# A chain of small elementwise steps placed on GpSimd instead of VectorE, in a two-layer hybrid decoder kernel

## The chip, the cores and the metric

The kernel runs on one core of one Trainium2 chip. The core's engines work side by side and wait for each other by semaphores: TensorE (PE in the profile) multiplies matrices, VectorE (DVE), ScalarE (ACT) and GpSimd (POOL) do elementwise work, SyncE (SP) issues transfers. The metric is the device time of one execution, in microseconds (us).

## The reference

One inference step of two layers, over a prompt of 512 tokens and 8 sequences of 4 new tokens, 1024 wide. In each layer the normalized input is multiplied by `w_in`, the columns of the product go to four mixers (SSD, retention, GLA, RG-LRU), their outputs through `w_out`, and a SwiGLU follows. The change touches how the SSD mixer gets its log decays, and two factors of the RG-LRU:

```python
dt = jax.nn.softplus(dt_raw.astype(jnp.float32) + p['ssd_dt_bias'].astype(jnp.float32))
log_a = -dt * jnp.exp(p['ssd_a_log'].astype(jnp.float32))
...
log_a = -LRU_C * r.astype(jnp.float32) * jax.nn.softplus(-p['lru_lambda'].astype(jnp.float32))
```

The kernel computes softplus(x) as max(x, 0) + log(1 + e), where e = exp(-|x|), and the logarithm as 2z(1 + z²/3 + z⁴/5 + ...) with z = e/(2 + e), up to z¹⁴/15. All of it is on tiles of 128 rows by 19 columns: 16 step sizes of the prompt's four chunks, one of the samples, two of the RG-LRU.

## The kernel before

Tokens lie along the free axis: 512 of the prompt and 32 samples, in two halves of 272. Weights come in units of 1024 x 128 (`NUNIT` = 101 a layer; 25 are `w_in`, `IN_UNITS`). Each unit is multiplied in fp32 precision from rounded parts, three matmuls for each of 8 slices and each half, all on L1238 (`unit_half`), so 24 matmuls make one half of one unit. A half stands in one of three PSUM banks until DVE has emptied it (`dense_free`).

A unit's weights need preparing in a ring of three. SP loads `raw` (L362). ACT rounds it to `wh` (L404). The rest `wl` is made in one of two ways: for units 3 to 24 of each layer (`ON_VECTOR`), ACT writes -wh to `wl` (L406, `negated`) and POOL issues an accumulating transfer of the same weights onto it (L383, `lo_added`). For the others POOL subtracts (L376). POOL walks the units in order and does nothing else.

The 25 units of `w_in` make 50 slots, two a unit (a unit and its half). Each engine goes through the slots in the same order: PE multiplies the half, DVE empties it (`evacuate`; for units 1 to 6 that is `conv`, a causal convolution, L717 to L735), ACT prepares the weights of the unit three ahead (`hi_ahead`). Between them stand the mixers' stages, by a table written out by hand (`SLOTS`). Three matter here:

- `dt` in slot 5. PE turns the step sizes (L1249, L1252), DVE adds the bias (L786 to L789, `sp_in`), ACT makes exp(-|x|) (L448 to L452, `sp_exp`), and DVE does the whole rest, L792 to L820, with a drain after each dependent step, and signals `dt_ready`.
- `gla_cum` in slot 9: DVE's L907 and the scans of L910.
- `ssd_a` of chunk 0 in slot 12: PE waits for `dt_ready` and `conv_silu`, then does L1315 and what follows. ACT's exponentials and DVE's L852 come after PE there.

Slot 6 begins with unit 3's first half. PE's next use of the bank that this half stands in, slot 9, needs DVE's L719 of slot 6, which is behind all of `dt` on DVE.

Of the kernel before, what the change touches and what calls it, by code (L numbers as in the profile page):

```python
# [25 lines left out]
ALU = mybir.AluOpType  # L26
ACT = mybir.ActivationFunctionType
F32 = mybir.dt.float32
F32R = mybir.dt.float32r

P = 128
# [37 lines left out]
NUNIT = REST0 + 2 * REST + KT  # L69
# [10 lines left out]
def splits(n):  # L80

    layer, u = divmod(n, NUNIT)
    vector = layer * len(ON_VECTOR) + min(max(u - 3, 0), len(ON_VECTOR))
    return (u in ON_VECTOR, vector + 1 if u in ON_VECTOR else n - vector)
# [89 lines left out]
def trunk(nc, weights, params, consts, x, s_ssd, s_ret, s_gla, y, o_conv, o_ssd, o_ret, o_gla, o_lru,  # L174
          n_ssd, n_ret, n_gla):
    with ExitStack() as ctx:
        def sb(name, cols, dt=F32, parts=P):
            return ctx.enter_context(nc.sbuf_tensor(name, [parts, *cols], dt))

        def sem(name):  # L180
            return ctx.enter_context(nc.semaphore(name))

        def signal(name, per_layer, start=0):
            return Signal(sem(name), per_layer, start)


        h = sb("h", [KT, TOK])
# [8 lines left out]
        sp_x, sp_a, sp_e, sp_z = (sb(n, [19]) for n in ("sp_x", "sp_a", "sp_e", "sp_z"))  # L196
        sp_2, sp_p, sp_m, sp_y = (sb(n, [19]) for n in ("sp_2", "sp_p", "sp_m", "sp_y"))
        ssd_rate, log_a, st_log_a = sb("ssd_rate", [5]), sb("log_a", [4, 4]), sb("st_log_a", [1])
        log_a_hi, log_a_lo = sb("log_a_hi", [4, 4], F32R), sb("log_a_lo", [4, 4], F32R)
        st_e, st_mask = sb("st_e", [2 * NSEQ + 2]), sb("st_mask", [NSEQ])  # L200
        lru_neg, lru_pos = sb("lru_neg", [2]), sb("lru_pos", [2])
# [58 lines left out]
        def par(name, i=0, n=1):  # L260
            at, _ = PARAM[name]
            return pr[:, at + i:at + i + n]
# [32 lines left out]
        act_lo = signal("act_lo", FT)  # L295

        dt_out, dt_turned, sp_in, sp_exp = (signal(n, 1) for n in ("dt_out", "dt_turned", "sp_in", "sp_exp"))
        dt_ready = signal("dt_ready", 1)
        conv_done = signal("conv_done", 6)
        conv_silu = signal("conv_silu", 4)  # L300
        ssd_a, ssd_e, ssd_dx, ssd_bin, ssd_b, ssd_s = (
# [44 lines left out]
        @block.sync  # L346
        def _(sp):
            sp.dma_start(raw[:, 0, :], weights[0]).then_inc(raw_loaded[0], 16)
            for i in range(KT // 2):
                sp.dma_start(h[:, 2 * i:2 * i + 2, :], x[:, 2 * i:2 * i + 2, :]).then_inc(x_loaded[i], 16)  # L350
            sp.wait_ge(x_loaded[1], 16)
            sp.dma_start(raw[:, 1, :], weights[1]).then_inc(raw_loaded[1], 16)
            sp.wait_ge(x_loaded[KT // 2 - 1], 16)
            sp.dma_start(raw[:, 2, :], weights[2]).then_inc(raw_loaded[2], 16)
            sp.dma_start(S1[:, 0:NEXACT], consts[:, NCONST + KT:NCONST + KT + NEXACT]).then_inc(exact_loaded, 16)
            sp.wait_ge(first_lo, 1)
            sp.dma_start(raw[:, 0, :], weights[3]).then_inc(raw_loaded[0], 16)
            sp.dma_start(cs[:], consts[:, 0:NCONST]).then_inc(consts_loaded, 16)
            for n in range(1, ALL - RING):
                vector, count = splits(n)  # L360
                sp.wait_ge(negated if vector else lo_done, count)
                sp.dma_start(raw[:, n % RING, :], weights[n + RING]).then_inc(raw_loaded[n % RING], 16)  # L362
            for s in range(RING):
                sp.wait_ge(raw_loaded[s], 16 * len(range(s, ALL, RING)))
            for i in range(KT // 2):
                sp.wait_ge(y_final, 2 * i + 2)
                sp.dma_start(y[:, 2 * i:2 * i + 2, :], h[:, 2 * i:2 * i + 2, :]).then_inc(y_stored, 16)
            sp.wait_ge(y_stored, 16 * (KT // 2))
            sp.wait_ge(stored, DEPTH * STORES)


        @block.gpsimd
        def _(pool):
            def split(s, n):
                pool.wait_ge(hi_done, n + 1)
                nc.gpsimd.tensor_tensor(wl[:, s, :], raw[:, s, :], wh[:, s, :].bitcast(F32),  # L376
                                        ALU.subtract).then_inc(lo_done, 1)

            for n in range(1, ALL):
                vector, count = splits(n)  # L380
                if vector:
                    pool.wait_ge(negated, count)
                    nc.gpsimd.dma_start(wl[:, n % RING, :], weights[n], accum_op=ALU.add).then_inc(lo_added[n % RING], 16)  # L383
                else:
                    split(n % RING, n)

# [2 lines left out]
        def _(act):  # L389
# [51 lines left out]
            for layer in range(DEPTH):  # L441
# [82 lines left out]
                def gla_b_(c):  # L524
                    _, off, n = CH[c]
                    act.wait_ge(gla_b.sem, gla_b.at(layer, c + 1))
                    for t in range(2):
                        ins = a(gv[:, t, off:off + n], M[2 - t if c < SAMPLE else 2 + t][:, 0:n], ACT.Copy)
                    ins.then_inc(gla_o.sem, 1)
# [123 lines left out]
        def _(dve):  # L653
            v = nc.vector
            tt, ts, stt, copy = v.tensor_tensor, v.tensor_scalar, v.scalar_tensor_tensor, v.tensor_copy
# [45 lines left out]
            for layer in range(DEPTH):  # L701
# [80 lines left out]
                def dt(_=None):  # L782
                    dve.wait_ge(dt_turned.sem, dt_turned.at(layer, 1))
                    dve.wait_ge(consts_loaded, 16)
                    bias = par("dt_bias", 0, 4)
                    tt(sp_x[:, 0:16].rearrange("p (c h) -> p c h", h=4), M[4][:, 0:16].rearrange("p (c h) -> p c h", h=4),  # L786
                       bias.unsqueeze(1).to_broadcast([P, 4, 4]), ALU.add)
                    tt(sp_x[:, 16:17], M[4][:, 16:17], par("dt_bias", 4), ALU.add)
                    ts(sp_x[:, 17:19], par("lru_lambda", 0, 2), -1.0, None, ALU.mult)  # L789
                    dve.drain().then_inc(sp_in.sem, 1)  # L790

                    ts(sp_m[:], sp_x[:], 0.0, None, ALU.max)  # L792
                    dve.wait_ge(sp_exp.sem, sp_exp.at(layer, 1))
                    ts(sp_z[:], sp_e[:], 2.0, None, ALU.add)
                    dve.drain()
                    v.reciprocal(sp_z[:], sp_z[:])
                    dve.drain()
                    tt(sp_z[:], sp_z[:], sp_e[:], ALU.mult)
                    dve.drain()
                    tt(sp_2[:], sp_z[:], sp_z[:], ALU.mult)  # L800
                    dve.drain()
                    ts(sp_p[:], sp_2[:], 1.0 / 15.0, None, ALU.mult)
                    for k in (13, 11, 9, 7, 5, 3):
                        dve.drain()
                        stt(sp_p[:], sp_p[:], 1.0 / k, sp_2[:], ALU.add, ALU.mult)
                    dve.drain()
                    stt(sp_p[:], sp_p[:], 1.0, sp_z[:], ALU.add, ALU.mult)
                    dve.drain()
                    stt(sp_y[:], sp_p[:], 2.0, sp_m[:], ALU.mult, ALU.add)
                    dve.drain()  # L810
                    stt(log_a[:], sp_y[:, 0:16].rearrange("p (c h) -> p c h", h=4), -1.0,
                        ssd_rate[:, 0:4].unsqueeze(1).to_broadcast([P, 4, 4]), ALU.mult, ALU.mult)
                    stt(st_log_a[:], sp_y[:, 16:17], -1.0, ssd_rate[:, 4:5], ALU.mult, ALU.mult)
                    dve.drain()
                    copy(log_a_hi[:], log_a[:])
                    dve.drain()
                    tt(log_a_lo[:], log_a[:], log_a_hi[:].bitcast(F32), ALU.subtract)
                    ts(lru_neg[:], sp_y[:, 17:19], -8.0, None, ALU.mult)
                    ts(lru_pos[:], sp_y[:, 17:19], 8.0, None, ALU.mult)
                    dve.drain().then_inc(dt_ready.sem, 1)  # L820

                def ssd_sample_stacks():
                    group = cst("pair").unsqueeze(1).unsqueeze(3).to_broadcast([P, 2, 2, NS])
# [291 lines left out]
                def ret_out(t):  # L1115
# [3 lines left out]

                stages = {  # L1120
                    "dt": dt, "ssd_a": ssd_a_, "ssd_b": ssd_b_, "lru_scan": lru_scan, "gla_cum": gla_cum,
                    "gla_pre": gla_pre_, "gla_a": gla_a_, "gla_b": gla_b_, "rotate": rotate, "ret_a": ret_a_,
                    "ret_b": ret_b_, "ret_out": ret_out, "z_gate": z_gate, "gla_stat": lambda: norm_rstd(0, 4, 64), "gla_norm": gla_norm_,
# [657 lines left out]
```

## Time and profile before

| | |
|---|---|
| median of 3 runs | 1423.91 us (1422.46 to 1425.79) |
| the profiled execution | 1419.99 us |
| its span, first to last instruction | 1418.2 us |
| PE busy (matmuls) | 1377.8 us, 97% |
| DVE busy | 640.0 us, 45% |
| ACT busy | 496.8 us, 35% |
| POOL busy | 415.5 us, 29% |
| mean granted clock of PE | 0.988 |

Matmuls are pipelined, so a busy PE isn't PE at its peak: the start-to-start distance of its rows says more. Busy shares are means over all stages; what a stage waits for is read in its own stretch of the timeline. Lines are those of the kernel before.

### The profile page before, as it was taken

To read this page: it belongs to the slowest core of one execution; us is meant where nothing else is said; L and a number is where in the kernel's file an instruction comes from. 1 tells how busy PE (TensorE), PEld (TensorE's weight loads), DVE (VectorE), ACT (ScalarE), POOL (GpSimd) and SP (SyncE) were. 2 spreads that over 40 slices of the span, in tenths; PEclk is the share of its full clock that TensorE was granted. 3 is DMA by queue.
4 is the path that set the end of the run, shared out by engine and by line. 5 is a ranking of instruction groups with operands and counts; after the bars stand their busy time and mean duration, and the time that the engine had idled before them with its cause. 6 is when DMAs were issued, how large, how long until landed. Compare 5 with 4: busy or idle time off the path is not lost.

```text
span 1418.2 us, 25863 instructions
## 1 busy us (share of the span) xinstructions
PE 1377.8 (97%) x11237; PEld 1331.4 (94%) x11237; DVE 640.0 (45%) x1230; ACT 496.8 (35%) x685; POOL 415.5 (29%) x205
## 2 busy tenths in 40 slices
PE   6998999999999999999999989999999999999996
PEld 6987888999999999999989878889999999999996
DVE  5744766464331333133756446755433223322334
ACT  5625354433221222122454264543322122212231
POOL 1100001343334444333511000024334444333441
PEclk9999999999999999999999999999999999999998
DMA  7644654222222222232355466423232222332221
GB/s 267 138 98 116 156 118 110 75 75 90 90 90 88 83 86 87 90 90 90 106 146 121 107 145 160 91 79 94 85 90 85 81 89 90 90 90 90 89 91 64
DMA packets 41347, 146.09 MB, mean 103 GB/s; under 512 B 5136, under 2 KB 6160, under 8 KB 41104
## 3 DMA queue, kind: packets, MB, share of 16 engines
q1 hardware_dynamic: 30528, 112.01, 26.2%
q0 software_dynamic: 6336, 23.07, 9.0%
q10 hardware_dynamic: 4368, 9.34, 2.1%
q8 instruction: 89, 1.46, 0.4%
q14 instruction: 26, 0.21, 0.0%
HBM read 136.35 MB, written 5.82 MB: 100 GB/s over the span
## 4 chain that ended last, share of the span: by engine, by line
PE 86%; DVE 5%; ACT 4%; DVEq 1%; DMA 1%; issue 1%; ACTq 1%; POOL 0%; SPq 0%
PE bank L1238 78%; PE bank L1188 1%; DMA wl<-weights 1%; PE bank L1478 1%; ACT wh L404 1%; PE bank L1329 0%; ACT wl L406 0%; PE bank L1204 0%; PE bank L1389 0%; ACT xh L429 0%; PE bank L1484 0%; ACT L487 0%; PE bank L1414 0%; DVE h L1179 0%; PE bank L1199 0%
## 5 line engine op out<-in xcount | busy, mean ns | idle before, releaser
L1238 PE MATMUL bank<-xh,wh 128*128 128x272 f32 x2208 | 651.3, 295 | 13.7 <-DVE xl L692 7.7
L1238 PE MATMUL bank<-xh,wl 128*128 128x272 f32 x2208 | 643.5, 291 | 0.0
L1238 PE MATMUL bank<-xl,wh 128*128 128x272 f32 x2208 | 639.7, 290 | 0.0
L376 POOL TENSOR_TENSOR wl<-raw,wh 128x1024 fp32r<-128x1024 f32 x157 | 377.0, 2402 | 590.7 <-ACT wh L404 574.8
L404 ACT ACTIVATE wh<-raw 128x1024 fp32r<-128x1024 f32 x199 | 210.8, 1059 | 693.1 <-PE bank L1238 672.2
L1238 PEld LDWEIGHTS bank<-xh,wh 128*128 128x128 f32 x2208 | 420.3, 190 | 20.9 <-issue 15.9
L1238 PEld LDWEIGHTS bank<-xl,wh 128*128 128x128 f32 x2208 | 421.1, 191 | 1.1 <-issue 0.5
L1238 PEld LDWEIGHTS bank<-xh,wl 128*128 128x128 f32 x2208 | 419.8, 190 | 0.0
L1157 DVE TENSOR_TENSOR tz<-bank,rs_bcast 128x272 f32<-128x272 f32 x176 | 77.5, 441 | 293.3 <-PE bank L1238 289.2
L1137 DVE TENSOR_TENSOR h<-h,bank 128x272 f32<-128x272 f32 x128 | 55.3, 436 | 215.8 <-PE bank L1238 215.8
L383 POOL DMA_DIRECT2D wl<-weights x44 | 38.3, 870 | 385.5 <-ACT wl L406 385.5
L1238 PE MATMUL bank<-gh_gla,wh 128*128 128x272 f32 x256 | 73.9, 289 | 1.0 <-DVE gl_gla L1165 1.0
L1238 PE MATMUL bank<-gh_ret,wl 128*128 128x272 f32 x256 | 74.4, 290 | 0.0
L1238 PE MATMUL bank<-gl_gla,wh 128*128 128x272 f32 x256 | 73.9, 289 | 0.0
L1238 PE MATMUL bank<-gh_ssd,wl 128*128 128x272 f32 x256 | 73.9, 289 | 0.0
L1238 PE MATMUL bank<-gl_ssd,wh 128*128 128x272 f32 x256 | 73.9, 289 | 0.0
L1238 PE MATMUL bank<-gh_ssd,wh 128*128 128x272 f32 x256 | 73.9, 289 | 0.0
L1238 PE MATMUL bank<-gh_gla,wl 128*128 128x272 f32 x256 | 73.8, 288 | 0.0
L1238 PE MATMUL bank<-gh_ret,wh 128*128 128x272 f32 x256 | 73.5, 287 | 0.0
L1238 PE MATMUL bank<-gl_ret,wh 128*128 128x272 f32 x256 | 73.4, 287 | 0.0
L672 DVE TENSOR_TENSOR sq_sum<-sq_sum,Vx 128x544 f32<-128x544 f32 x30 | 61.4, 2048 | 4.6 <-issue 1.3
L1238 PE MATMUL bank<-gh_lru,wl 128*128 128x272 f32 x192 | 55.9, 291 | 0.0
(360 smaller groups left out, 1763.2 us busy)
## 6 DMA issues: line engine op xcount, KB each, us to landing
raw<-weights SPq DMA_DIRECT2D x202, 512.0 KB, 3.6
wl<-weights POOLq DMA_DIRECT2D x44, 512.0 KB, 7.6
h<-x SPq DMA_DIRECT2D x4, 544.0 KB, 6.0
y<-h SPq DMA_DIRECT2D x4, 544.0 KB, 2.7
cs<-consts SPq DMA_DIRECT2D x1, 1336.5 KB, 8.2
rv<-rk ACTq DMA_DIRECT2D x8, 136.0 KB, 5.8
tz<-rq ACTq DMA_DIRECT2D x8, 136.0 KB, 4.7
S<-s_ssd ACTq DMA_DIRECT2D x2, 512.0 KB, 4.3
```

The lines of the kernel that those rows point to most:

```text
L376: nc.gpsimd.tensor_tensor(wl[:, s, :], raw[:, s, :], wh[:, s, :].bitcast(F32), ALU.subtract).then_inc(lo_done, 1)
L383: nc.gpsimd.dma_start(wl[:, n % RING, :], weights[n], accum_op=ALU.add).then_inc(lo_added[n % RING], 16)
L404: a(wh[:, s, :], raw[:, s, :], ACT.Copy).then_inc(hi_done, 1)
L672: tt(sq_sum[:], sq_sum[:], sq[:, m % 2, :], ALU.add).then_inc(sq_added.sem, 1)
L1137: ins = tt(h[:, m, cols], h[:, m, cols], acc, ALU.add)
L1157: tt(tz[:, i // 2, cols], acc, rs_bcast[:, cols], ALU.mult).then_inc(dense_free.sem, 1)
L1188: return nc.tensor.transpose(out, src, exact("ident", n_in, 0, n_in).bitcast(F32))
L1238: ins = mm(bank_, wt[:, n % RING, w], xx[:, cols], start=(i == 0 and j == 0), stop=(i == len(ks) - 1 and j == 2))
L1478: ins = mm(M[4][0:n, at:at + 2], sq[:, t, off:off + n], cst("pair"), start=True, stop=True)
```

## The change

ScalarE's part of `dt` stays. VectorE keeps the bias, 2 + e, and the reciprocal, and signals `sp_recip`. Everything behind that, and max(x, 0), is done by GpSimd in a new function `step_sizes`, called once a layer: right behind the transfer issue of unit 6, so ahead of the wait and issue for unit 7. The fused steps of VectorE (`scalar_tensor_tensor`, one instruction) are two instructions on GpSimd, an add or a multiply by a constant and one of two tensors. Its last drain signals `dt_ready`.

```diff
--- before.py
+++ after.py
@@ -295,7 +295,7 @@
         act_lo = signal("act_lo", FT)
 
         dt_out, dt_turned, sp_in, sp_exp = (signal(n, 1) for n in ("dt_out", "dt_turned", "sp_in", "sp_exp"))
-        dt_ready = signal("dt_ready", 1)
+        dt_ready, sp_recip = signal("dt_ready", 1), signal("sp_recip", 1)
         conv_done = signal("conv_done", 6)
         conv_silu = signal("conv_silu", 4)
         ssd_a, ssd_e, ssd_dx, ssd_bin, ssd_b, ssd_s = (
@@ -376,11 +376,47 @@
                 nc.gpsimd.tensor_tensor(wl[:, s, :], raw[:, s, :], wh[:, s, :].bitcast(F32),
                                         ALU.subtract).then_inc(lo_done, 1)
 
+            def step_sizes(layer):
+                pool.wait_ge(sp_in.sem, sp_in.at(layer, 1))
+                nc.gpsimd.tensor_scalar(sp_m[:], sp_x[:], 0.0, None, ALU.max)
+                pool.wait_ge(sp_recip.sem, sp_recip.at(layer, 1))
+                nc.gpsimd.tensor_tensor(sp_z[:], sp_z[:], sp_e[:], ALU.mult)
+                pool.drain()
+                nc.gpsimd.tensor_tensor(sp_2[:], sp_z[:], sp_z[:], ALU.mult)
+                pool.drain()
+                nc.gpsimd.tensor_scalar(sp_p[:], sp_2[:], 1.0 / 15.0, None, ALU.mult)
+                for k in (13, 11, 9, 7, 5, 3):
+                    pool.drain()
+                    nc.gpsimd.tensor_scalar(sp_p[:], sp_p[:], 1.0 / k, None, ALU.add)
+                    pool.drain()
+                    nc.gpsimd.tensor_tensor(sp_p[:], sp_p[:], sp_2[:], ALU.mult)
+                pool.drain()
+                nc.gpsimd.tensor_scalar(sp_p[:], sp_p[:], 2.0, 2.0, ALU.mult, ALU.add)
+                pool.drain()
+                nc.gpsimd.tensor_tensor(sp_p[:], sp_p[:], sp_z[:], ALU.mult)
+                pool.drain()
+                nc.gpsimd.tensor_tensor(sp_y[:], sp_p[:], sp_m[:], ALU.add)
+                pool.drain()
+                nc.gpsimd.tensor_scalar(sp_m[:], sp_y[:], -1.0, None, ALU.mult)
+                pool.drain()
+                nc.gpsimd.tensor_tensor(log_a[:], sp_m[:, 0:16].rearrange("p (c h) -> p c h", h=4),
+                                        ssd_rate[:, 0:4].unsqueeze(1).to_broadcast([P, 4, 4]), ALU.mult)
+                nc.gpsimd.tensor_tensor(st_log_a[:], sp_m[:, 16:17], ssd_rate[:, 4:5], ALU.mult)
+                pool.drain()
+                nc.gpsimd.tensor_copy(log_a_hi[:], log_a[:])
+                pool.drain()
+                nc.gpsimd.tensor_tensor(log_a_lo[:], log_a[:], log_a_hi[:].bitcast(F32), ALU.subtract)
+                nc.gpsimd.tensor_scalar(lru_neg[:], sp_y[:, 17:19], -8.0, None, ALU.mult)
+                nc.gpsimd.tensor_scalar(lru_pos[:], sp_y[:, 17:19], 8.0, None, ALU.mult)
+                pool.drain().then_inc(dt_ready.sem, 1)
+
             for n in range(1, ALL):
                 vector, count = splits(n)
                 if vector:
                     pool.wait_ge(negated, count)
                     nc.gpsimd.dma_start(wl[:, n % RING, :], weights[n], accum_op=ALU.add).then_inc(lo_added[n % RING], 16)
+                    if n % NUNIT == 6:
+                        step_sizes(n // NUNIT)
                 else:
                     split(n % RING, n)
 
@@ -788,36 +824,11 @@
                     tt(sp_x[:, 16:17], M[4][:, 16:17], par("dt_bias", 4), ALU.add)
                     ts(sp_x[:, 17:19], par("lru_lambda", 0, 2), -1.0, None, ALU.mult)
                     dve.drain().then_inc(sp_in.sem, 1)
-
-                    ts(sp_m[:], sp_x[:], 0.0, None, ALU.max)
                     dve.wait_ge(sp_exp.sem, sp_exp.at(layer, 1))
                     ts(sp_z[:], sp_e[:], 2.0, None, ALU.add)
                     dve.drain()
-                    v.reciprocal(sp_z[:], sp_z[:])
-                    dve.drain()
-                    tt(sp_z[:], sp_z[:], sp_e[:], ALU.mult)
-                    dve.drain()
-                    tt(sp_2[:], sp_z[:], sp_z[:], ALU.mult)
-                    dve.drain()
-                    ts(sp_p[:], sp_2[:], 1.0 / 15.0, None, ALU.mult)
-                    for k in (13, 11, 9, 7, 5, 3):
-                        dve.drain()
-                        stt(sp_p[:], sp_p[:], 1.0 / k, sp_2[:], ALU.add, ALU.mult)
-                    dve.drain()
-                    stt(sp_p[:], sp_p[:], 1.0, sp_z[:], ALU.add, ALU.mult)
-                    dve.drain()
-                    stt(sp_y[:], sp_p[:], 2.0, sp_m[:], ALU.mult, ALU.add)
-                    dve.drain()
-                    stt(log_a[:], sp_y[:, 0:16].rearrange("p (c h) -> p c h", h=4), -1.0,
-                        ssd_rate[:, 0:4].unsqueeze(1).to_broadcast([P, 4, 4]), ALU.mult, ALU.mult)
-                    stt(st_log_a[:], sp_y[:, 16:17], -1.0, ssd_rate[:, 4:5], ALU.mult, ALU.mult)
-                    dve.drain()
-                    copy(log_a_hi[:], log_a[:])
-                    dve.drain()
-                    tt(log_a_lo[:], log_a[:], log_a_hi[:].bitcast(F32), ALU.subtract)
-                    ts(lru_neg[:], sp_y[:, 17:19], -8.0, None, ALU.mult)
-                    ts(lru_pos[:], sp_y[:, 17:19], 8.0, None, ALU.mult)
-                    dve.drain().then_inc(dt_ready.sem, 1)
+                    v.reciprocal(sp_z[:], sp_z[:]).then_inc(sp_recip.sem, 1)
+
 
                 def ssd_sample_stacks():
                     group = cst("pair").unsqueeze(1).unsqueeze(3).to_broadcast([P, 2, 2, NS])
```

POOL's order in the build, after the change, layer 0, with the semaphores that it waits for (`sp_2` is printed as `sp`):

```order
L376 TENSOR_TENSOR wl<-raw,wh 128x1024 [waits hi_done] x2
L417 DMA wl<-weights 128x1024 [waits negated] x4
L381 TENSOR_SCALAR sp_m<-sp_x 128x19 [waits sp_in]
L383 TENSOR_TENSOR sp_z<-sp_z,sp_e 128x19 [waits sp_recip]
L385 TENSOR_TENSOR sp<-sp_z 128x19
L387 TENSOR_SCALAR sp_p<-sp 128x19
L390 TENSOR_SCALAR sp_p<-sp_p 128x19
L392 TENSOR_TENSOR sp_p<-sp_p,sp 128x19
...
L408 TENSOR_TENSOR log_a_lo<-log_a,log_a_hi 128x16
L409 TENSOR_SCALAR lru_neg<-sp_y 128x2
L410 TENSOR_SCALAR lru_pos<-sp_y 128x2
L417 DMA wl<-weights 128x1024 [waits negated] x18
```

Before, the issues of all 22 units followed each other (`L383 DMA ... x22`); now 26 instructions stand behind the fourth.

DVE's order before, from the bias in slot 5 to the evacuation in slot 6:

```order
L789 TENSOR_SCALAR sp_x<-pr 128x2
L792 TENSOR_SCALAR sp_m<-sp_x 128x19
L794 TENSOR_SCALAR sp_z<-sp_e 128x19 [waits sp_exp]
L796 RECIPROCAL sp_z<-sp_z 128x19
L798 TENSOR_TENSOR sp_z<-sp_z,sp_e 128x19
...
L819 TENSOR_SCALAR lru_pos<-sp_y 128x2
L717 MEMSET cbuf 128x3 [waits dense_done]
L718 COPY cbuf<-pr 128x8x3
L719 TENSOR_TENSOR cbuf<-bank,rs_bcast 128x272
```

and after:

```order
L825 TENSOR_SCALAR sp_x<-pr 128x2
L828 TENSOR_SCALAR sp_z<-sp_e 128x19 [waits sp_exp]
L830 RECIPROCAL sp_z<-sp_z 128x19
L753 MEMSET cbuf 128x3 [waits dense_done]
L754 COPY cbuf<-pr 128x8x3
L755 TENSOR_TENSOR cbuf<-bank,rs_bcast 128x272
```

Eighteen instructions have left DVE between the reciprocal's neighbourhood and the evacuation, which now follows the reciprocal at once.

## Rows read from the trace of the kernel before

**Rows 1.** Page, the chain that ended last: share of the span by engine
```profile
PE 86%; DVE 5%; ACT 4%; DVEq 1%; DMA 1%; issue 1%; ACTq 1%; POOL 0%; SPq 0%
```

**Rows 2.** Timeline of DVE, layer 0: start us, duration us, instruction, [idle before <- releaser]
```profile
44.61 0.17 DVE L794 TENSOR_SCALAR sp_z<-sp_e 128x19 f32<-128x19 f32 x1 [2.21 <-ACT sp_e L452]
...
44.86 0.28 DVE L796 RECIPROCAL sp_z<-sp_z 128x19 f32<-128x19 f32 x1
...
45.21 0.18 DVE L798 TENSOR_TENSOR sp_z<-sp_z,sp_e 128x19 f32<-128x19 f32 x1
...
49.05 0.18 DVE L718 COPY cbuf<-pr 128x24 f32<-128x24 f32 x1
```

**Rows 3.** Timeline of PE, layer 0, around unit 4's second half and at chunk 1
```profile
48.85 0.28 PE L1238 MATMUL bank<-xh,wl 128*128 128x272 f32 x1
...
49.62 0.39 PE L1238 MATMUL bank<-xh,wh 128*128 128x272 f32 x1 [0.49 <-DVE cbuf L719]
...
73.33 0.66 PE L1315 MATMUL bank<-cx,log_a 128*64 128x128 f32 x8 [0.71 <-DVEq L883]
```

**Rows 4.** Chain of waits in layer 1: start us, length us, what
```profile
724.89 8.49 DMA wl<-weights
...
740.41 18.30 PE bank L1238 x144
```

**Rows 5.** Timeline of DVE, layer 1: its waits for PE
```profile
743.65 0.41 DVE L722 TENSOR_TENSOR cbuf<-bank,rs_bcast 128x240 f32<-128x240 f32 x1 [2.00 <-PE bank L1238]
...
762.16 0.42 DVE L852 TENSOR_TENSOR V<-bank,sp_y 128x256 f32<-128x256 f32 x1 [1.34 <-PE bank L1188]
```

**Rows 6.** Timeline of POOL: the transfer issues of unit 6, layers 0 and 1
```profile
50.98 0.86 POOL L383 DMA_DIRECT2D wl<-weights  x1 [10.26 <-ACT wl L406]
...
746.96 0.88 POOL L383 DMA_DIRECT2D wl<-weights  x1 [13.51 <-ACT wl L406]
```

**Rows 7.** L383, transfers issued at 56.46, then at 752.04 (unit 7)
```profile
DMA to landing us min/median/max: 8.1/8.1/8.1
...
DMA to landing us min/median/max: 7.5/7.5/7.5
```

**Rows 8.** Timeline of PE: start of ssd_a(0) and of unit 7
```profile
61.89 0.44 PE L1315 MATMUL bank<-cx,log_a 128*64 128x128 f32 x4
...
69.25 0.47 PE L1238 MATMUL bank<-xh,wh 128*128 128x272 f32 x1
...
758.64 0.66 PE L1315 MATMUL bank<-cx,log_a 128*64 128x128 f32 x8
...
765.99 0.47 PE L1238 MATMUL bank<-xh,wh 128*128 128x272 f32 x1
```

**Rows 9.** One line each: instruction xcount: duration ns min/median/max, first and last start
```profile
L376 POOL TENSOR_TENSOR wl<-raw,wh x157: 2372/2398/2671, 14.0 to 1389.5; 128x1024 fp32r<-128x1024 f32 x157
...
L842 DVE TENSOR_TENSOR Vx<-S,st_e x2: 1224/1224/1225, 112.9 to 809.6; 128x1024 f32<-128x1024 f32 x2
...
L1757 POOL MEMSET const-float32-0.0<- x1: 98/98/98, 0.2 to 0.2; 128x1 f32 x1
...
L684 DVE MEMSET sp_x<- x1: 74/74/74, 0.8 to 0.8; 128x19 f32 x1
```

**Rows 10.** Timelines of DVE, then POOL, where two-input work meets L376
```profile
479.46 0.72 DVE L1162 TENSOR_TENSOR tz<-tz 128x544 f32<-128x544 f32 x1 [0.44 <-issue]
...
480.91 2.12 DVE L1165 TENSOR_TENSOR gl_ssd<-tz,gh_ssd 128x544 fp32r<-128x544 f32 x1 [0.73 <-ACT gh_ssd L635]
...
479.77 2.67 POOL L376 TENSOR_TENSOR wl<-raw,wh 128x1024 fp32r<-128x1024 f32 x1 [3.64 <-ACT wh L404]
```

**Rows 11.** Timeline of DVE, layer 0: the fourth convolution's passes
```profile
55.23 2.58 DVE L735 SCALAR_TENSOR_TENSOR ct<-cbuf,pr,ct 128x568 f32<-128x568 f32 x3
```

**Rows 12.** Timeline of PE; then a stretch: us, busy by engine, PEclk, DMA share, GB/s
```profile
32.70 0.59 PE L1238 MATMUL bank<-xh,wh 128*128 128x272 f32 x1 [2.50 <-DVE cbuf L719]
...
32.70:36.00 3.30, 3.30 (x14) 3.30 (x15) 2.99 (x8) 0.00 (x0) 0.00 (x0) 0.50 1.01 243
```

## The prediction

> **What bounds the kernel now.** I read the page first: the chain that ended last is TensorE (PE) for 86% of the span, almost all of it on the matmuls of L1238, with VectorE (DVE) on 5% [rows 1]. So an edit on DVE or GpSimd (POOL) moves the time only where PE waits, and I looked for those places around the `dt` stage of each layer, in the list of waits, then in the timelines of PE, DVE and POOL, then in the chain of waits. The median of the runs is 1423.91 us; the profiled execution took 1419.99 us (span 1418.2), 3.9 below it. The sum is made against that execution, and 3.9 is added for the median. A change of under 0.2% (2.85 us) can't be told from none here.
>
> In layer 0, DVE does the chain from L798 to L819 between 45.21 and 49.05 us, and only then empties the bank that PE needs [rows 2]. PE issues a matmul every 0.125 us; here it goes from 48.85 to 49.62, so it loses 0.77 - 0.12 = 0.65 us [rows 3]. In layer 1 it loses nothing: it waits for a transfer until 733.38 and from 740.41 computes 144 matmuls without a break, up to `ssd_a` [rows 4], and DVE, through with the chain, waits 2.00 us for PE at L722 [rows 5].
>
> **What the change removes.** 18 DVE instructions a layer, 3.84 us of the timeline in layer 0. In layer 0 PE then waits for nothing at that bank: **-0.65 us**. Beyond that DVE is early for nothing: it waits for PE again soon. In layer 1: **0**. The reciprocal and the wait for ScalarE's exponential (2.21 us, [rows 2]) stay on DVE, ahead of the bank.
>
> **What it adds: a chain on POOL.** It stands behind the transfer issue of unit 6 and ahead of that of unit 7. It has two kinds of wait, for `sp_in` and `sp_recip`; both are met some 6 us before POOL gets there (DVE's reciprocal ends at 45.14; the issue of unit 6 starts at 50.98, held by ScalarE [rows 2, 6]). So the chain starts at 50.98 + 0.86 = 51.84, and in layer 1 at 746.96 + 0.88 = 747.84. ScalarE's work before it doesn't come from DVE's chain, so I leave these as they are.
>
> Two things wait for its end. PE's `ssd_a(0)` waits for `dt_ready`: PE is there at 61.89, or 61.24 with the 0.65 gained, and in layer 1 at 758.64 [rows 8]. That leaves **9.4 and 10.8 us**. The transfer of unit 7, queued behind on POOL, takes 8.1 us from issue to landing in layer 0 and 7.5 in layer 1 [rows 7], and PE starts that unit at 69.25 - 0.65 = 68.60 and at 765.99 [rows 8]. It must be issued by 60.5 and 758.5, so the chain may take **8.7 and 10.65 us**. The unit after is needed a whole unit of PE later and has the room. SP's queue waits on ScalarE's `negated`, not on POOL, so the raw loads don't move.
>
> How long is the chain? 26 instructions a layer, of which 22 follow each other with a drain between and 4 don't. The trace has no small two-sided instruction on POOL. Bounds for one drained step: from below, a POOL MEMSET of 0.10 us plus the 0.08 that DVE leaves between drained instructions (44.61 + 0.17 to 44.86), 0.18. From above, POOL takes 2.40 us for 1024 elements; if it ran at DVE's pace (1.22 - 0.18 us for 1005 more elements, 1.04 ns each), 1.33 us of that would be fixed, so about 1.4 [rows 2, 9]. That end is not likely: the whole ratio of POOL to DVE at 1024 elements is 2.40/1.22 = 1.96, which makes of DVE's 0.18 us some 0.35, and 0.43 with the gap; the MEMSETs (98 against 74 ns) have a ratio of 1.3, which makes 0.31. I take 0.36, between but nearer to the small forms, as these are small. With a MEMSET's 0.1 for each of the other four, 22 x 0.36 + 4 x 0.1 = **8.3 us** with nothing in the way.
>
> Something is in the way. At 479.77 the POOL instruction of L376 took 2.67 us instead of 2.40, when DVE had begun one with two SBUF inputs 0.31 us before; and the next of DVE's, L1165, took 2.12 us beside it, where the same shape at L1162 took 0.72 [rows 9, 10]. Whoever comes second waits for the first to end. In the chain's window DVE has such work: three passes of L735 for 2.58 us [rows 11], L907 and the scans of L910, and L732 before them; in layer 0 they now follow PE's unit 4 closely and so come a little earlier than in these rows, but still in the window. During L735's passes (one each 0.86 us) POOL gets about one step in each, and loses 3 x (0.86 - 0.36) = 1.5 us; I give L732, L907 and the five scans 0.7 together. Bounds: 0, and the 1.5 twice (the next convolution follows) with 0.2 for each of those seven, about 4.4. I take 2.2, and the chain lasts **10.5 us**.
>
> The Trainium skill says the same of this place (SBUF — State Buffer, "SBUF: two separate sides"): the pair of ports that VectorE and GpSimd share is locked for a whole instruction, and the other blocks. It speaks against the move; the trace agrees, with the 2.67 against 2.40 us. Without the rule the chain would be the 8.3 us above and the sum -0.65.
>
> **The sum.** Layer 0: the chain ends at 51.84 + 10.5 = 62.34, 1.10 after PE wants it. Unit 7's transfer is issued then and lands at 70.45; PE, late by 1.10, comes at 69.70 and waits 0.75. -0.65 + 1.10 + 0.75 = +1.2. Layer 1: the chain ends at 758.34, before 758.64; the transfer lands at 765.85, before 765.99: 0. DVE itself may lose up to 0.3 us for each instruction that meets a POOL step; it has the 3.84 us in layer 0, and in layer 1 it still waits 1.34 us for PE at L852 [rows 5], so 0. Total **+1.2 us**: 1421.2 for an execution like the profiled one, a median of **1425.1**.
>
> **The rivals.**
> *The chain is hidden whole.* If it takes under 8.7 us, all that is left is -0.65: 1423.3. For it: 0.31 a step and 1.0 for DVE's work give 8.2. Against: the 2.67 and 2.12 us [rows 10]. Chance 0.15.
> *The chain is the new bound (slower).* Place: PE at `ssd_a(0)` in both layers. From 11.4 us on (a step of 0.40 with the 2.2 for DVE) it costs over 2.85 us. At a step of 0.47 the chain is 13 us: layer 0 pays 64.84 - 61.24 = 3.6, 0.75 and -0.65; layer 1 pays 2.2 and 0.15 for the transfer. That is 6.1, and after the PE wait of 2.50 us before 32.70 the granted clock was 0.50, the lower level, for 3.3 us, with 14 matmuls, which take 1.75 us at 0.125 each [rows 12], so about 1.6 more in layer 0: +7.7, 1431.6. For it: the ratio 1.96 gives 0.43 already. Chance 0.27.
> *A cost at the first use.* POOL has run no TENSOR_SCALAR nor CAST before layer 0's chain. A one-off start, if there is one, adds to layer 0 alone, a microsecond of PE for each. Nothing in the rows prices it; as long as POOL's longest instruction, 2.67 us [rows 9], it makes +3.9, 1427.8. Against: the first TENSOR_TENSOR on POOL, at 14.0, is within the 2.37 to 2.67 us of all 157 [rows 9]. Chance 0.06. The Trainium skill (GPSIMD Engine Reference, "Instruction dispatch") puts the first call of a freshly loaded kernel at about 6 us with no row of its own; by that figure the sum would be some +7, an estimate near 1431. No run here shows it.
> *DVE's freed time is worth more.* DVE is also waited for at the next chunk (PE's 0.7 us at L1315 on DVE's L883, [rows 3]). If an early DVE removes that in both layers too, -0.65 - 2 x 0.7 = -2.05: 1421.9. Against: DVE waits for PE at L722 just before, so it isn't late with old work. Chance 0.04.
> The forecast itself, a chain of 8.7 to 11.4 us, has 0.45; 0.03 is for what I don't see.
>
> **How the numbers follow.** The forecast's band runs from -0.65 to +2.85, 1423.3 to 1426.8. The range takes in the hidden case with the spread of the three runs below it, and the slow chain at 13 us: 1422.0 to 1432.0. Slower by over 0.2%: the 0.27, most of the first-use case (0.04) and the top of the forecast's band with measurement (0.04), 0.35. Faster: 0.05. Same: 0.60.
>
> **What would show it.** On POOL: the distance from sp_m's first to lru_pos' last row (10.5 us), the step between two sp_p rows (0.36 where DVE is idle, about 0.85 beside L735's passes). On DVE: the bank of the third convolution emptied before PE asks, no PE wait near 49. On PE: a wait of 1.1 us at L1315 in layer 0 and none in layer 1, and 0.7 at the start of unit 7. I'm wrong if the step on POOL is 0.2 or over 0.45, if the chain doesn't start right behind the issue, or if PE waits at 49 as before.

## The result, and the profile after

| | before | changed |
|---|---|---|
| median | 1423.18 us (1421.59 to 1425.79, 4 runs) | 1446.67 us (1444.58 to 1449.56, 4 runs) |
| profiled execution | 1419.99 us | 1449.56 us |
| its span | 1418.2 us | 1447.7 us |
| mean granted clock of PE | 0.988 | 0.975 |

The changed kernel takes 1.0167 of the time before (95% interval 1.0142 to 1.0192): **23.5 us slower**. The prediction said 1425.1, with 1422.0 to 1432.0 as its range. The profiled execution of the change is the slowest of its four runs, that of before lies 3.2 us below its median, so the two traces differ by 29.6; which part of that is the change is worked out below.

The list of what PE waited for over the whole of the changed kernel has one new name on top:

```profile
PE bank L1326 <- POOLq L411: 15.8, 2, 8.4
...
PE bank L1249 <- DMA wl<-weights: 3.2, 2, 1.6
...
PE bank L1249 <- DVE cbuf L755: 2.5, 1, 2.5
```

(line, what for: us in total, times, longest.) L1326 is `ssd_a(0)`, L1315 before; L411 is the last drain of `step_sizes`. So PE waits twice, once a layer, for the end of the chain, some 8 us each where 1.1 and 0 were predicted. The wait of 0.49 us for VectorE near 49 us [rows 3] is gone: the two waits for `cbuf` (3.0 us before) are one of 2.5, and one of 0.4 us for another part of `cbuf` (L759) has come up, at 37.6 us. The wait of 1.6 us in layer 0 for `wl` is for unit 6's transfer, at 58.79 us; the kernel before had no wait there.

Why the chain ends late is on POOL's timeline in layer 0 (start us, us, instruction, [idle before <- releaser]):

```profile
50.48 0.86 POOL L417 DMA_DIRECT2D wl<-weights  x1 [10.00 <-ACT wl L442]
51.05 0.62 POOL L381 TENSOR_SCALAR sp_m<-sp_x 128x19 f32<-128x19 f32 x1
51.29 0.57 POOL L383 TENSOR_TENSOR sp_z<-sp_z,sp_e 128x19 f32<-128x19 f32 x1
58.96 0.38 POOL L385 TENSOR_TENSOR sp<-sp_z 128x19 f32<-128x19 f32 x1 [7.11 <-issue]
59.50 0.81 POOL L387 TENSOR_SCALAR sp_p<-sp 128x19 f32<-128x19 f32 x1 [0.16 <-issue]
...
62.18 0.27 POOL L390 TENSOR_SCALAR sp_p<-sp_p 128x19 f32<-128x19 f32 x1 [0.16 <-issue]
62.60 0.23 POOL L392 TENSOR_TENSOR sp_p<-sp_p,sp 128x19 f32<-128x19 f32 x1
62.98 0.27 POOL L390 TENSOR_SCALAR sp_p<-sp_p 128x19 f32<-128x19 f32 x1 [0.16 <-issue]
...
69.19 0.22 POOL L410 TENSOR_SCALAR lru_pos<-sp_y 128x2 f32<-128x2 f32 x1
69.99 1.84 POOL L417 DMA_DIRECT2D wl<-weights  x2 [0.58 <-issue]
```

The chain does start right behind unit 6's issue, with the two operations that have no drain ahead of them, L381 and L383. Then comes the first drain of the chain (L384), and the square z^2 behind it starts **7.11 us** after L383's end. The later drains leave 0.14 to 0.16 us (one in layer 1 leaves 0.46). Layer 1 has the same hold at the same place:

```profile
762.19 0.57 POOL L383 TENSOR_TENSOR sp_z<-sp_z,sp_e 128x19 f32<-128x19 f32 x1
770.45 0.22 POOL L385 TENSOR_TENSOR sp<-sp_z 128x19 f32<-128x19 f32 x1 [7.69 <-issue]
...
781.21 0.22 POOL L410 TENSOR_SCALAR lru_pos<-sp_y 128x2 f32<-128x2 f32 x1
```

"issue" says that the engine waited for nothing that this view shows; drains have no row in it. In the record of single instructions the drain at L384 lasts 8.32 us in layer 0. What ends near it is unit 6's transfer. Its issue at 50.48 answers with:

```profile
DMA to landing us min/median/max: 8.2/8.2/8.2
```

which is 58.7, and z^2 starts at 58.96. That made the first theory.

PE after the stall, in stretches (us, busy by engine, granted clock, DMA share, GB/s):

```profile
66.00:72.00 6.00, 2.49 (x12) 1.98 (x13) 0.00 (x0) 0.00 (x0) 4.08 (x13) 0.50 0.09 7
72.00:78.00 6.00, 6.00 (x28) 5.56 (x27) 1.94 (x5) 1.11 (x4) 0.00 (x0) 0.50 0.88 168
78.00:84.00 6.00, 6.00 (x44) 5.62 (x43) 3.04 (x8) 2.01 (x2) 0.87 (x1) 0.86 0.13 12
```

The granted clock is at its lower level, 1.2 GHz, until about 80 us. The same work, from the start of `ssd_a(0)` to that of unit 7, took 7.36 us before and takes 11.96 here.

**Where the 23.5 us are.** PE's start of `ssd_a(0)` and of unit 7, which before are at 61.89, 69.25 and at 758.64, 765.99 [rows 8], are now

```profile
69.51 1.12 PE L1326 MATMUL bank<-cx,log_a 128*64 128x128 f32 x8 [7.45 <-POOLq L411]
...
81.47 0.48 PE L1249 MATMUL bank<-xh,wh 128*128 128x272 f32 x1
...
781.53 0.69 PE L1326 MATMUL bank<-cx,log_a 128*64 128x128 f32 x4 [8.38 <-POOLq L411]
...
792.57 0.47 PE L1249 MATMUL bank<-xh,wh 128*128 128x272 f32 x1
```

Layer 0: 7.6 us late at `ssd_a(0)`, 12.2 at unit 7; the 4.6 between are the lower clock. PE came to `ssd_a(0)` at 62.06 and not at 61.24; it had waited 1.56 us for unit 6's transfer. Layer 1: by its wait of 8.38 us PE got to `ssd_a(0)` at 773.15, so 14.5 us late, began it 22.9 late and was 26.6 late at unit 7: 12.1 more, 3.7 of them the lower clock. Together the two stages cost **24.3 us**. The other 5 of the 29.6 were not followed row by row. The changed kernel has stretches at the lower clock elsewhere that the profiled execution of before has not, or has shorter (at 141, 199, 909 and 933 us of its own timeline). The version without the chain, which measures as before, has such stretches at the same places of the program, so they aren't charged to the change.

### The profile page after: what moved, and what is told of

Its sections match the earlier page's. It is cut to its first block, busy times and chain, and to the rows that moved or that the text cites. A ratio compares the mean times of both kernels' runs of the same rounds, so it can differ in the third digit from the quotient of the medians.

```text
span 1447.7 us, 25893 instructions
## 1 busy us (share of the span) xinstructions
PE 1390.5 (96%) x11237; PEld 1342.2 (93%) x11237; DVE 634.9 (44%) x1194; ACT 496.9 (34%) x685; POOL 431.3 (30%) x257
## 4 chain that ended last, share of the span: by engine, by line
PE 84%; DVE 5%; ACT 4%; issue 2%; DVEq 1%; POOLq 1%; ACTq 1%; DMA 1%; POOL 0%; SPq 0%
PE bank L1249 74%; PE bank L1199 1%; PE bank L1489 1%; PE bank L1340 1%; ACT wh L440 1%; DMA wl<-weights 1%; ACT wl L442 1%; PE bank L1400 0%; PE bank L1215 0%; PE bank L1326 0%; PE bank L1495 0%; ACT xh L465 0%; POOLq L391 0%; POOLq L389 0%; DVE h L1190 0%
## 5 line engine op out<-in xcount | busy, mean ns | idle before, releaser
L1249 PE MATMUL bank<-xh,wh 128*128 128x272 f32 x2208 | 654.1, 296 | 14.7 <-DVE xl L728 7.7
L376 POOL TENSOR_TENSOR wl<-raw,wh 128x1024 fp32r<-128x1024 f32 x157 | 376.7, 2400 | 591.1 <-ACT wh L440 575.1
```

Source lines behind the costliest of these rows:

```text
L1249: ins = mm(bank_, wt[:, n % RING, w], xx[:, cols], start=(i == 0 and j == 0), stop=(i == len(ks) - 1 and j == 2))
```

## The experiments

The theories they were set against:

- **A**: a drain on GpSimd ends only when the transfer issued ahead of it on GpSimd has landed.
- **B**: code of GpSimd is loaded at its first use; in its second form, **B'**, the first drain behind an issue costs a fixed 7 us.
- **C**: GpSimd is busy with the transfer's descriptors for some us behind the issue.
- **D**: the chain is simply too long, with its 22 steps and the port that it shares with VectorE.

### A drain behind every transfer issue of the kernel before

Behind each of the 44 issues GpSimd drains and writes one column of a tile of its own, so that the drain's end has a row.

```diff
                     nc.gpsimd.dma_start(wl[:, n % RING, :], weights[n], accum_op=ALU.add).then_inc(lo_added[n % RING], 16)
+                    pool.drain()
+                    nc.gpsimd.memset(mark[:], 0.0)
```

> The kernel before, with a drain and a one-column MEMSET on GpSimd behind each of the 44 accumulating transfer issues; VectorE keeps its chain. The MEMSET's row marks when the drain lets go. If a drain on GpSimd waits until the transfer issued ahead of it has landed (theory A), the MEMSETs come 7 to 9 us after each issue, with the 6.2 to 9.8 us that the landings scatter over, in both layers and also in stages where VectorE is idle. If the 7 us of the changed kernel were code fetched at the first use of a new kind of instruction (B), the MEMSETs come within 1.5 us everywhere. If GpSimd is busy writing descriptors (C), they come at 7 us here and in the next kernel too. The time: unit 7's issue in layer 0 moves from 56.5 to about 59 us and is in time, so within 4 us of before; a few of the closer pairs of issues (units 3 and 4) are pushed apart, up to 10 us more by A.

POOL's timeline in layer 0:

```profile
28.38 1.01 POOL L384 DMA_DIRECT2D wl<-weights  x1 [7.33 <-ACT wl L409]
37.68 0.09 POOL L386 MEMSET mark<- 128x1 f32 x1 [8.28 <-issue]
38.12 0.86 POOL L384 DMA_DIRECT2D wl<-weights  x1 [0.35 <-ACT wl L409]
45.64 0.10 POOL L386 MEMSET mark<- 128x1 f32 x1 [6.65 <-issue]
46.08 0.86 POOL L384 DMA_DIRECT2D wl<-weights  x1 [0.35 <-issue]
51.96 0.10 POOL L386 MEMSET mark<- 128x1 f32 x1 [5.01 <-issue]
```

and the landing of the issues at 28.38 and 38.12:

```profile
DMA to landing us min/median/max: 9.1/9.1/9.1
```

```profile
DMA to landing us min/median/max: 7.4/7.4/7.4
```

28.38 + 9.1 = 37.5, 38.12 + 7.4 = 45.5: the MEMSETs stand at 37.68 and 45.64. In the records of single instructions the last landing of each of the 44 issues comes 5.5 to 9.1 us behind the issue, and in all 44 the drain ends 0.07 to 0.08 us after it. A fixed cost couldn't follow the landings over 3.6 us. The drain doesn't wait for SyncE's transfers: one of `raw`, issued at 49.82, took 3.5 us to land, and the drain behind the issue at 46.08 had let go by 51.96. **A holds, D alone falls, and so does B**: there is no chain and no new kind of operation here, and the hold is there each time.

The same MEMSETs without the drain weren't measured, so that C is left to the next version. The time was 1417.37 us in its one run, against 1423.1 (1417.44 to 1427.19, 13 runs) for before: one run shows no cost of 44 such holds, where nothing behind the drain is wanted soon. The issues of units 4 to 8 come late here, and PE waits for none of their transfers.

### The chain without drains

Each drain of the chain is replaced by a semaphore that the operation raises and the next one waits for; the operations and their place stay. The last three raise `dt_ready` themselves, without a drain behind them.

```diff
+            def after_step(ins):
+                stepped[0] += 1
+                ins.then_inc(sp_step, 1)
+                pool.wait_ge(sp_step, stepped[0])
...
-                nc.gpsimd.tensor_tensor(sp_z[:], sp_z[:], sp_e[:], ALU.mult)
-                pool.drain()
-                nc.gpsimd.tensor_tensor(sp_2[:], sp_z[:], sp_z[:], ALU.mult)
-                pool.drain()
+                after_step(nc.gpsimd.tensor_tensor(sp_z[:], sp_z[:], sp_e[:], ALU.mult))
+                after_step(nc.gpsimd.tensor_tensor(sp_2[:], sp_z[:], sp_z[:], ALU.mult))
```

> The changed kernel, with each drain in the chain replaced by a wait on a semaphore that the step before increments; same instructions, same place. A: no hold of 7 us behind the first product, a step of 0.35 to 0.45 us, the chain ends some 9 to 11 us after the issue of unit 6, and PE waits 0 to 2 us at ssd_a(0) in each layer: the time is within 3 us of before. B or C: the hold of 7 us stays and the time stays near 1446. If the chain's length and the shared port are what costs (D), the time stays over 1435.

1431.11 us (1425.55 to 1435.14, 10 runs), 1.005 of before (1.0029 to 1.007): two thirds of the loss are gone, and 8.0 us are left, where A alone had allowed 3. POOL in layer 0:

```profile
51.07 0.86 POOL L415 DMA_DIRECT2D wl<-weights  x1 [10.28 <-ACT wl L440]
...
51.87 0.57 POOL L391 TENSOR_TENSOR sp_z<-sp_z,sp_e 128x19 f32<-128x19 f32 x1
52.52 0.22 POOL L392 TENSOR_TENSOR sp<-sp_z 128x19 f32<-128x19 f32 x1
...
54.67 0.84 POOL L395 TENSOR_SCALAR sp_p<-sp_p 128x19 f32<-128x19 f32 x1
55.59 0.76 POOL L396 TENSOR_TENSOR sp_p<-sp_p,sp 128x19 f32<-128x19 f32 x1
...
58.21 0.27 POOL L395 TENSOR_SCALAR sp_p<-sp_p 128x19 f32<-128x19 f32 x1
58.56 0.23 POOL L396 TENSOR_TENSOR sp_p<-sp_p,sp 128x19 f32<-128x19 f32 x1
58.88 0.27 POOL L395 TENSOR_SCALAR sp_p<-sp_p 128x19 f32<-128x19 f32 x1
...
63.81 0.22 POOL L409 TENSOR_SCALAR lru_pos<-sp_y 128x2 f32<-128x2 f32 x1
```

z^2 follows 0.08 us behind z*e while unit 6's transfer is under way. So GpSimd isn't busy with the transfer: **C falls**, and it is the drain that waits, not the engine. What is left is D: the chain, 51.63 to 64.03, takes **12.4 us**, in layer 1 (748.56 to 761.54) **13.0**, against the 9.4 and 10.8 of room. A step without VectorE is 0.335 us (two from 58.21 to 58.88); ten of the rows in layer 0 take 0.3 to 0.86 us instead of 0.2 to 0.3, together 4.0 us too much, in layer 1 4.5. They stand where VectorE makes its passes of two inputs, so these are the port's. Without them the chain would be 8.4 and 8.5 us long, an estimate from these rows, and would fit both rooms. PE waits for it less than for the drain, but it waits, in layer 0, then in layer 1:

```profile
64.08 0.66 PE L1324 MATMUL bank<-cx,log_a 128*64 128x128 f32 x8 [1.40 <-POOL lru_pos L409]
...
761.59 0.66 PE L1324 MATMUL bank<-cx,log_a 128*64 128x128 f32 x8 [1.86 <-POOL lru_pos L409]
```

Unit 7's transfer, issued at 761.60 and so 3.1 us after the latest time of the prediction, costs nothing: it lands 5.5 us later, before PE comes to that unit at 772.0. The rest is the clock. In layer 1 it is at its lower level for 6.8 us from 763.5 us on, and from `ssd_a(0)` to unit 7 PE takes 10.4 us, 3.1 more than before:

```profile
765.00:778.00 13.00, 11.94 (x78) 10.87 (x77) 6.89 (x17) 3.12 (x6) 0.86 (x1) 0.80 0.62 130
```

### The chain ahead of unit 6's issue

```diff
             for n in range(1, ALL):
                 vector, count = splits(n)
                 if vector:
+                    if n % NUNIT == 6:
+                        step_sizes(n // NUNIT)
                     pool.wait_ge(negated, count)
                     nc.gpsimd.dma_start(wl[:, n % RING, :], weights[n], accum_op=ALU.add).then_inc(lo_added[n % RING], 16)
-                    if n % NUNIT == 6:
-                        step_sizes(n // NUNIT)
```

> The changed kernel with its drains, the chain called ahead of the wait and issue for unit 6 in place of behind it. The transfer in flight is then unit 5's, landed about 3 us after the chain's start in each layer. A: a hold of 3 us, then 8 to 9 us of steps; the chain ends at about 56 us in layer 0 and 749 in layer 1, dt_ready is in time, but unit 6's transfer is issued 5 us late in layer 0 and lands at 63 or 64 where PE wants it at 58: PE waits 4 to 6 us there, 0 to 2 in layer 1: 1428 to 1433 us. B: a hold of 7 us here as well, 1440 or more. C: as A. D: over 1435.

1441.44 us (1437.97 to 1445.7, 4 runs), 1.0142 of before (1.0097 to 1.0186); I had this version too fast. POOL and PE in layer 0:

```profile
43.03 0.23 POOL L383 TENSOR_TENSOR sp_z<-sp_z,sp_e 128x19 f32<-128x19 f32 x1 [2.73 <-DVE sp_z L830]
46.18 0.22 POOL L385 TENSOR_TENSOR sp<-sp_z 128x19 f32<-128x19 f32 x1 [2.92 <-issue]
...
58.37 0.24 POOL L410 TENSOR_SCALAR lru_pos<-sp_y 128x2 f32<-128x2 f32 x1
59.20 2.73 POOL L419 DMA_DIRECT2D wl<-weights  x3 [0.58 <-issue]
```

```profile
64.70 0.57 PE L1249 MATMUL bank<-xh,wh 128*128 128x272 f32 x1 [6.22 <-DMA wl<-weights]
```

The drain holds here too, but for 2.92 us (3.45 in layer 1), since unit 5's transfer is 5.3 us old when z*e ends: A once more, with another unit. The chain then blocks the queue: unit 6 is issued at 59.20, 8.2 us after its time [rows 6], and PE waits 6.22 us for it. `ssd_a(0)` doesn't wait for the chain, and the loss is 18 us against the changed kernel's 23.5. In layer 1 the wait for unit 6's transfer is 4.25 us, where 0 to 2 had been expected: the chain there, begun at 745.59, ends only at 762.05.

### The chain later behind the same issue

The call stands behind the wait for unit 7's `negated`, ahead of its issue.

```diff
                     pool.wait_ge(negated, count)
+                    if n % NUNIT == 7:
+                        step_sizes(n // NUNIT)
                     nc.gpsimd.dma_start(wl[:, n % RING, :], weights[n], accum_op=ALU.add).then_inc(lo_added[n % RING], 16)
-                    if n % NUNIT == 6:
-                        step_sizes(n // NUNIT)
```

> The changed kernel with the chain called behind the wait for unit 7's negation and ahead of unit 7's issue, so that it starts some 4 us later behind unit 6's issue. Theory A (a drain on GpSimd ends when the transfer issued ahead of it has landed): the hold between z*e and z^2 is shorter by as much as the chain starts later, and z^2 begins at the same 59 us in layer 0 and 770.5 us in layer 1 as in the changed kernel; time as the changed kernel, 1441 to 1450 us. Theory B' (a fixed cost of about 7 us of the first drain behind an issue, whatever the age of the transfer): z^2 begins some 4 us later than in the changed kernel, at about 63 us, and the time is 6 to 10 us above the changed kernel. Theory D (the length of the chain alone): no hold at all; excluded if either is seen.

```profile
50.85 0.86 POOL L419 DMA_DIRECT2D wl<-weights  x1 [10.28 <-ACT wl L442]
54.61 0.66 POOL L381 TENSOR_SCALAR sp_m<-sp_x 128x19 f32<-128x19 f32 x1 [2.90 <-ACT wl L442]
55.25 0.22 POOL L383 TENSOR_TENSOR sp_z<-sp_z,sp_e 128x19 f32<-128x19 f32 x1
59.24 0.22 POOL L385 TENSOR_TENSOR sp<-sp_z 128x19 f32<-128x19 f32 x1 [3.77 <-issue]
```

Begun 3.6 us later, the chain is let go at the same time, 59.24 (predicted 59; 58.96 in the changed kernel). The hold is 3.77 us, not 7: **B' falls**. In layer 1 it is 3.17, 9.06 us behind the issue as in the changed kernel (770.45 - 761.38 = 9.07); z^2 stands there at 763.96 and not at the 770.5 expected, as unit 6's issue itself comes 6.5 us earlier (754.90). Time: 1443.13 us in its one run, between the bounds of A.

### What the move could be worth at most

The chain's arithmetic is left out: GpSimd writes constants into its seven results.

```diff
             def step_sizes(layer):
-                pool.wait_ge(sp_in.sem, sp_in.at(layer, 1))
-                nc.gpsimd.tensor_scalar(sp_m[:], sp_x[:], 0.0, None, ALU.max)
                 pool.wait_ge(sp_recip.sem, sp_recip.at(layer, 1))
...
+                for out, value in ((sp_y, 0.01), (log_a, -2.0 ** -7), (st_log_a, -2.0 ** -7), (log_a_hi, -2.0 ** -7), (log_a_lo, 0.0),
+                                   (lru_neg, -0.01), (lru_pos, 0.01)):
+                    nc.gpsimd.memset(out[:].bitcast(F32), value).then_inc(dt_ready.sem, 1)
```

> The changed kernel without the chain's arithmetic: behind unit 6's issue GpSimd writes constants into the seven tiles that the chain made, with one signal each; the computation from step sizes to log decays is left out, so that this is the most that taking the chain from VectorE can be worth. My price of the freed VectorE time is 0.65 us (the bank freed earlier near 49 us in layer 0), so 1422.5 us against 1423.2, within 0.2%. If GpSimd's chain were harmless and the loss came from elsewhere in the change (sp_z and sp_recip handed over, other order), it would be as slow as the changed kernel, 1440 and above. A gain of over 3 us would say that VectorE's chain cost more than the trace showed.

1423.76 us (1420.36 to 1430.85, 12 runs) against 1422.77 (1416.15 to 1429.03, 29 runs), a ratio of 1.0005 (0.9988 to 1.0023). All of the loss is in the chain on GpSimd: the handing over and the new order cost nothing that shows. A chain that cost nothing would bring nothing that can be measured. The chain of waits of its profiled execution (start us, length us, what) has the half microsecond at the bank gone:

```profile
43.43 18.30 PE bank L1221 x144
```

144 matmuls without a break, through the place where PE lost 0.65 us before. So the wait at the bank is gone, as the prediction had it, and what that is worth is too small for twelve runs.

### The same gain without GpSimd

The kernel before, with the chain left on VectorE but put behind the evacuation at slot 6.

```diff
 at_slot(5, "dt")
+at_slot(6, "dt_rest")
...
                     dve.drain().then_inc(sp_in.sem, 1)
 
+                def dt_rest(_=None):
                     ts(sp_m[:], sp_x[:], 0.0, None, ALU.max)
```

> The kernel before, with the chain left on VectorE but moved from slot 5 behind the two operations at slot 6, so that the bank is freed ahead of it. Expected by the trace of before: the 0.49 us wait of PE near 49 us goes, nothing else moves, log decays are ready by about 52 us, 9 us before PE wants them: 1422.5 us, within 0.2% of before. Rival: the later end of the scans behind it costs PE something (the two evacuations at slots 7 and 8 come 3 to 4 us later at most), 1424 to 1426 us.

1423.2 us (1419.63 to 1426.72, 12 runs), 0.9999 of before (0.9985 to 1.0014): no change. The wait near 49 is gone as expected. But the chain of waits has a piece that before didn't have:

```profile
50.49 0.28 issue
50.78 8.01 DMA wl<-weights
58.78 0.14 issue
58.92 1.12 PE bank L1240 x7
```

PE, earlier at unit 6, waits 0.96 us for its transfer. That is issued at 50.78, when ScalarE is through, whatever VectorE does, and took 8.0 us to land; in the changed kernel it took 8.2, and PE lost 1.56 us there, in the version with semaphores 8.2 and 1.14 us. The trace of before had 6.2, the version without the chain 6.4, and neither waited at this unit. Why it takes 6.2 in one execution and 8.2 in another isn't settled by these runs. The median shows no gain, nor the 1 to 3 us of the rival.

### The chain without drains, in two parts around unit 6's issue

From the version with semaphores. Ahead of unit 6's wait and issue stand `sp_m` and the next 13 operations in layer 0, `sp_m` and the next 3 in layer 1; the others stay behind the issue.

```diff
                 if vector:
+                    if n % NUNIT == 6:
+                        first_steps(n // NUNIT)
+                        terms((13, 11, 9, 7, 5) if n < NUNIT else ())
                     pool.wait_ge(negated, count)
                     nc.gpsimd.dma_start(wl[:, n % RING, :], weights[n], accum_op=ALU.add).then_inc(lo_added[n % RING], 16)
                     if n % NUNIT == 6:
-                        step_sizes(n // NUNIT)
+                        terms((3,) if n < NUNIT else (13, 11, 9, 7, 5, 3))
+                        last_steps(n // NUNIT)
```

> The kernel with semaphores in place of drains, and the chain in two parts around unit 6's issue: in layer 0 the first 13 operations ahead of it (GpSimd waits there for 7 us anyway), in layer 1 the first 3 ones. Theory A with the length of the chain as second term (12.4 us in layer 0 and 13.2 us in layer 1 from its first operation to its last, in the run with semaphores, against a room of 9.4 and 10.8 us): layer 0 now fits (8 us left behind the issue) and its PE wait on the chain goes; layer 1 keeps 11.6 us behind the issue and loses about 1 to 2 us; 1423 to 1427 us against 1431.1 with the chain in one piece. If the loss of the version with semaphores were not the chain's length but the issue queue or VectorE's shared port, the split changes nothing: 1429 to 1433 us.

1424.67 us (1418.19 to 1428.07, 10 runs), 1.0012 of before (0.9991 to 1.0032), against 1431.11 in one piece. PE waits for the chain in neither layer: in layer 1, where 1 to 2 us had been expected, what was left ran behind the issue in 9.4 us (747.97 to 757.33), since only about six of its operations met VectorE's passes. That the chain's length against the room was the second term is shown: with the waits for it, 6.4 us of the time went. How much of the length is the steps and how much the port, the split doesn't tell, as both got shorter. That this version is any better or worse than before isn't shown.

## Why the prediction was wrong

It forecast no change that could be told and had 0.35 on slower; the time was 21.6 us above the forecast and 14.7 above the range. Step by step:

- **"So the chain starts at 51.84 ... 8.3 us with nothing in the way" failed.** This step took the drain behind z*e, with the transfer just issued, to cost what DVE's drains cost, 0.08 us. The first of them held for the landing of unit 6's transfer, which moved the rest of the chain to 58.96 and 770.45, 7.1 and 7.7 us late. The landing time was in the prediction, 8.1 us [rows 7], but only as unit 7's price. The kernel before has no drain right behind an issue on GpSimd, so no row could show it; the bounds for one drained step should have had the landing as the upper bound of that first drain, being the one thing pending on the engine. Made so, with the prediction's own 10.5 less its first two operations (0.1 and 0.36), the sum is 50.98 + 8.1 + 10.0 = 69.1 for the chain's end in layer 0 (69.41 measured) and a PE wait of 7.8 (69.1 - 61.24; 7.45 measured). The 4.6 us of lower clock behind it would still be missing.
- **The step of 0.36 us** was 0.40 (62.18 to 62.98 is two): right within what it was given, over 22 steps 0.9 us. The ratio of POOL to DVE (0.43) was the better guide than the MEMSETs (0.31). A drain on GpSimd leaves 0.15 us with nothing in flight, where DVE's 0.08 had been taken.
- **2.2 us for the shared port** was 4.0 and 4.5 in the version where the chain meets the same passes as foreseen. The mechanism is as described: the operations beside L771's passes took 0.68 to 0.81 us. Not three but up to ten operations met them, as the next convolution's passes follow; that was the 4.4 of the upper bound. In the changed kernel itself the port costs less, some 1.6 and 1.8 us, since its PE, and so its VectorE, stands still for most of the chain.
- **The rival "new bound, 13 us, 1431.6"** names what happens without the drains: a chain of 12.4 and 13.0 us that PE waits for in both layers, and a lower clock behind it. That the time, 1431.11, agrees to half a microsecond is luck. The rival's 13 us were steps of 0.47 and 2.2 for the port, measured were 0.335 and 4.0 to 4.5; it had PE waiting 3.6 and 2.2 us for the chain (1.40 and 1.86 measured), 0.9 for unit 7's transfer (none) and 1.6 of lower clock in layer 0 (none there, 3.1 in layer 1), and no wait of 1.14 for unit 6. The kernel that was predicted, with its drains, lies 15.1 us above that rival (1446.67 - 1431.6): the hold and the clock behind it aren't in it.
- **0.75 us for unit 7's transfer** came in no version. Issued late, it landed in 5.4 us (changed kernel) and 5.8 us (semaphores) in layer 0 and not in 8.1, before PE came to the unit.
- **-0.65 us for the bank** was seen at the bank and lost again at unit 6's transfer. The prediction asked only DVE what is late next, and not the transfer behind ScalarE. The two versions made for it measured 1.0 and 0.4 us above before, both within the uncertainty.
- **Layer 1 at 0** failed as layer 0 did, by the same drain: 8.38 us. It would have failed without the drain too, by 1.86 us.
- **1.6 us of half clock** in the rival was 4.6 in layer 0 and 3.7 in layer 1, since PE stood 7 to 8 us and not 2.5. No such term was in the forecast.
- **A first-use cost** wasn't there: the instructions right behind the issue run at once, the version with semaphores runs the same kinds without a hold, and layer 1 has the hold as well. The figure of the Trainium skill (GPSIMD Engine Reference, "Instruction dispatch"), about 6 us for the first call of a freshly loaded kernel, is near the 7.1, and nearness is all that spoke for it.

## What to carry to other kernels

A drain on GpSimd, where that engine also issues transfers, isn't a flush of 0.1 us: it costs what is left of the transfer, up to the 5.5 to 9.1 us here when it stands right behind the issue, and 2.9 to 3.8 when the operation ahead of it ends 4.6 to 5.9 us behind the issue. On GpSimd, order dependent small operations by semaphores (0.335 us a step instead of 0.40, and no hold), or put the drains where nothing is in flight; and when work goes onto an engine that issues transfers, ask which of its instructions wait for everything pending. Before work is moved off an engine for a wait of half a microsecond, look at what PE meets next: leaving the chain out whole brought nothing.

## What was not expected

- The hold itself: 44 of 44 drains ended 0.07 to 0.08 us after the last landing of a transfer of 512 KB, 5.5 to 9.1 us behind its issue. That held with the issue directly ahead. In the three versions with drains inside the chain z^2 starts 0.26 to 0.3 us after the landing in layer 0, and in all three 1.03 us after it in layer 1. Where that last 0.75 us comes from wasn't tried. A drain can also hold with no transfer of GpSimd in flight: the one at the very end of the kernel before ends 3.7 us after the last operation on GpSimd (1391.91 to 1395.60), and no run here says why.
- PE's wait of 7.45 us was followed by some 10 us at the lower clock, which cost 4.6 us more: the stall's price was 1.6 times its length (1.4 times in layer 1). In the version without drains, whose waits in layer 0 were 1.1 and 1.4 us, the granted clock stayed at 1.00 there; in layer 1, behind a wait of 1.86 us, it fell all the same and cost 3.1 us. So the price of a wait isn't in proportion to it.
